# Two transformer blocks on one NeuronCore: attention steps regrouped among the products of the convolution units

## What is computed

```python
def hybrid_mixer(h, w_in, ...):
    proj = h @ w_in                      # 28 column groups of 128, and 8 gate columns
    aq, ak, av, dn_qkv, dn_z, dn_b, dn_a = jnp.split(proj, cuts, axis=-1)
    attn_out = dilated_attention(rope(aq), rope(ak), av)      # 8 heads of 64
    qkv = jax.nn.silu(causal_dwconv(dn_qkv, dn_conv_w))       # 12 of the 28 groups
    o = gated_delta_rule(dq, dk, dv, beta, g)
    return jnp.concatenate([attn_out, dn_out], axis=-1) @ w_out
```

## Time and profile before

| | |
|---|---|
| time, median of 3 runs | 2760.77 us (2760.47 to 2763.85) |
| the profiled execution's own time | 2765.85 us |
| its span | 2764.1 us (1.75 us lie around it) |
| TensorE busy | 97% of the span |
| ScalarE, VectorE, GpSimd busy | 40%, 40%, 44% |
| chain of work that ended last | 87% TensorE, 61% the unit's matmul line L1961 |
| conv units 13 to 23 in the trace | about 104 to 207 us (layer one), 742 us later again (layer two) |

### The profile page before, as it was taken

How to read it: one execution, slowest core, us unless ns; L and a number is a source line. 1 busy time by engine, 2 the same in 40 slices (tenths; PEclk the granted TensorE clock), 3 DMA queues, 4 the chain that set the end, 5 groups by cost and what they waited for, 6 DMA issues and landing times.

```text
span 2764.1 us, 42821 instructions
## 1 busy us (share of the span) xinstructions
PE 2685.1 (97%) x15208; PEld 2112.3 (76%) x15208; DVE 1098.6 (40%) x2260; ACT 1102.5 (40%) x1871; POOL 1211.5 (44%) x630
## 2 busy tenths in 40 slices
PE   9999999999999999999999999999999999999997
PEld 7767777888877677788887666788888666788886
DVE  4455454441154553644402586510113586510112
ACT  4454254443345533544434235532333235532331
POOL 3323235555433232355544452464653452364653
PEclk9999999999999999999999999999999999999998
DMA  3211023333322100233232221133332221133332
GB/s 136 77 54 40 9 77 91 99 93 105 106 71 69 54 25 24 78 97 96 94 106 92 71 69 47 62 99 99 92 98 84 71 69 47 61 97 94 99 93 97
DMA packets 62867, 217.16 MB, mean 79 GB/s; under 512 B 6576, under 2 KB 6704, under 8 KB 62480
## 3 DMA queue, kind: packets, MB, share of 16 engines
q1 hardware_dynamic: 62416, 214.28, 24.7%
q0 software_dynamic: 320, 1.12, 0.2%
HBM read 213.28 MB, written 2.10 MB: 78 GB/s over the span
## 4 chain that ended last, share of the span: by engine, by line
PE 87%; DVE 5%; ACT 2%; issue 2%; DVEq 2%; POOL 1%; DMA 0%; ACTq 0%; SPq 0%; POOLq 0%
PE bank L1961 61%; PE bank L2337 3%; PE bank L2011 3%; PE bank L2190 2%; PE bank L2191 2%; PE bank L2192 2%; PE bank L2023 1%; PE bank L2222 1%; PE bank L2234 1%; PE bank L2245 1%; PE bank L2127 1%; PE bank L1995 1%; PE bank L2356 1%; DVE mT L1786 1%; PE bank L1988 1%
## 5 line engine op out<-in xcount | busy, mean ns | idle before, releaser
L788 POOL TENSOR_TENSOR wL<-raw,wH 128x1024 fp32r<-128x1024 f32 x371 | 893.1, 2408 | 1085.5 <-ACT wH L977 1085.4
L1961 PE MATMUL bank<-hH,wH 128*128 128x512 f32 x1680 | 679.8, 405 | 7.0 <-DVE mT L1786 4.2
L1961 PE MATMUL bank<-hL,wH 128*128 128x512 f32 x1680 | 657.9, 392 | 0.0
L1961 PE MATMUL bank<-hH,wL 128*128 128x512 f32 x1680 | 657.5, 391 | 0.0
L977 ACT ACTIVATE wH<-raw 128x1024 fp32r<-128x1024 f32 x371 | 392.2, 1057 | 531.1 <-PE bank L1961 490.8
L1961 PEld LDWEIGHTS bank<-hH,wH 128*128 128x128 f32 x1680 | 317.1, 189 | 102.4 <-issue 28.8
L1961 PEld LDWEIGHTS bank<-hH,wL 128*128 128x128 f32 x1680 | 317.3, 189 | 67.5 <-issue 6.0
L1961 PEld LDWEIGHTS bank<-hL,wH 128*128 128x128 f32 x1680 | 316.9, 189 | 67.8
L1961 PE MATMUL bank<-hidH,wH 128*128 128x512 f32 x864 | 336.7, 390 | 0.0
L1961 PE MATMUL bank<-hidH,wL 128*128 128x512 f32 x864 | 336.2, 389 | 0.0
L1961 PE MATMUL bank<-hidL,wH 128*128 128x512 f32 x864 | 336.1, 389 | 0.0
(11 more groups left out here) (378 smaller groups left out, 3629.9 us busy)
## 6 DMA issues: line engine op xcount, KB each, us to landing
raw<-w_dram SPq DMA_DIRECT2D x398, 512.0 KB, 3.5
x<-x_dram SPq DMA_DIRECT2D x4, 512.0 KB, 9.6
out_dram<-x SPq DMA_DIRECT2D x1, 2048.0 KB, 6.3
const<-const_dram SPq DMA_DIRECT2D x1, 1229.0 KB, 13.2
par_next<-par_dram POOLq DMA_DIRECT2D x5, 168.0 KB, 3.5
qkT<-pos_dram POOLq DMA_DIRECT2D x1, 256.0 KB, 7.3
const<-const_dram SPq DMA_DIRECT2D x1, 131.0 KB, 2.2
```

The source lines that it names most:

```text
L788: pool.tensor_tensor(wL[:, s, :], raw[:, s, :], wH[:, s, :].bitcast(F32), ALU.subtract).then_inc(w_lo.sem, 1)
L1961: mm = pe.matmul((out or ACC[bk])[:, :], wt[:, c:c + P], rhs, start=first and k == 0 and j == 0, stop=last and k == tiles - 1 and j == 2)
```

## The change

TensorE's table of steps for a conv unit comes from a function instead of the fixed places 0, 3 and 6, and a place may hold more than one step. ScalarE's and VectorE's programs are not touched.

```diff
+def steps_in(v):
+
+    if v not in ATT_AT:
+        return {}
+    a, b, c = ATT_AT[v]
+    return {1: (a, b), 6: (c,)} if a % 2 else {0: (a,), 4: (b, c)}
...
-                    if k in after:
-                        attention(w, after[k])
+                    for n in after.get(k, ()):
+                        attention(w, n)
...
-                             after=dict(zip((0, 3, 6), ATT_AT.get(u, ()))))
+                             after=steps_in(u))
```

## The result

The changed kernel takes 2778.63 us (median of 5 runs, 2775.34 to 2778.71); the kernel before took 2762.91 us in the same session (5 runs, 2760.47 to 2767.95). The ratio is 1.0052 with a 95% interval of 1.0041 to 1.0063: by the ratio, slower by 14.4 us, 11.3 to 17.4 (the two medians are 15.7 us apart). The forecast was 14.0 us more, 2774.8 us, in a range of 2767 to 2783.

A forecast was written before the change was run, and what follows sets the result against it. TensorE, busy 104.1 of 105 us in each attention stage, was taken as the bound; even units 5.26 plus odd units 1.74 gave 7.00 us a layer, 14.0 in all, on 2760.8: 2774.8 us, range 2767 to 2783.

The forecast's parts named there:

- What bounds the stage: Attention stages: TensorE works 104.1 of 105 us in each, so whatever it waits in addition goes on the end.
- An even unit grows by its six products less the air: Units 14 to 22: six products of 0.23 us, 1.38 us, less each unit's air; 5.26 us a layer.
- The air method: Even units: second transposes' old start less copy's end plus 0.14 us; air of 0.01 to 0.40 us.
- Unit 22's old waits: Units 22 and 23: old waits of 0.46 and 0.18 us absorbed, so unit 22's 1.37 us becomes 0.73.
- Odd units: Pair behind k = 4: 0.57 us in unit 13, 0.92 in 23, 0.25 in the other four; 1.74 a layer.
- new neighbours: At each pair: coming to the scores from transposes instead of from a product costs about 0.03 us.
- Hidden: Even units: ScalarE's copy comes ahead of the pair, so the wait vanishes; 2760.2 us, no change; 5 in 100.
- Fewer breaks in the stream: One place less in each unit saves a toll, 22 x 0.22 = 4.8 us; 2754.7 us; 3 in 100.
- The clock falls: Behind the fourteen new waits the clock falls, 1.3 us each; all of them 18 us more, 2793; 8 in 100.
- The sum: Both layers' attention stages: 5.26 + 1.74 = 7.00 us a layer, 14.0 us in all, 2774.8 us, 0.5% slower.

The follow-up runs named there:

- odd-units kernel: Against the changed kernel, even units go back to steps behind k = 0, 3 and 6; only odd units keep the pair, behind k = 4: 2768.72 us, ratio 1.0019.
- two kernels with as many places as the change and few waits: Against the changed kernel: pairs behind k = 3 (even) and 6 (odd), 2766.61 us; ScalarE's weight high part moved behind its first attention step, 2768.81 us.
- the kernel with waits up to 0.82 us: Against the changed kernel, even pairs behind k = 0, odd units as before the change, ScalarE's weight high part behind its first attention step: 2771.77 us, ratio 1.0031.
- the kernel of before with ScalarE's edit: Against the kernel before, only ScalarE's high part of the weight moved behind the first attention step of its slots: 2762.23 us, ratio 1.0000.
- The kernel with the even units alone: Against the changed kernel, odd units go back to steps behind k = 0, 3 and 6; even units keep the pair behind k = 1: 2774.05 us, ratio 1.0037.

## Why the prediction was right, point by point

**What bounds the stage.** Right: TensorE, with no air. Every wait that the change made went on the end; nothing of it came back.

**An even unit grows by its six products less the air.** Right to 0.02 us in four units of five. The air method needs two rows of before for each unit, the end of the copy plus 0.14 us and the start of the transposes. It assumed that ScalarE's chain stays in place. The copy of unit 16 shows it, and the edit that moved the copy by 0.94 us took as much off the waits.

**Unit 22's old waits.** The largest error, 0.73 forecast and 0.54 measured, 0.4 us in two layers. I gave back what stood in the brackets, 0.46 + 0.18. Start to start the first was worth 0.66. The place with the four transposes of the earlier trace rows took from 193.70 to 195.25 us, 1.09 us more than two products; with the same transposes and no wait it took from 198.37 to 199.26 us in the changed trace, 0.43 us more.

**Odd units.** Units 13 and 23 right to 0.03 us. The odd-units kernel shows them alone. The 0.25 for the other four was 0.10: 0.09 in unit 19, where I had 0.13, and next to nothing in the three others, where I had 0.12 for new neighbours.

**The rivals.** *Hidden* is refuted: seven waits a layer. *Fewer breaks in the stream* is refuted by two kernels with as many places as the change and few waits (4.1 and 5.8 us slower, where the rows show 3.2 and 3.8 us of added waits and steps); a place less was worth 0.05 us a unit at most, not 0.22. The Trainium skill, "Perfetto Trace Analysis", section "Matmul Optimizations", asks for matmuls back to back in batches; longer batches are what these two kernels had, at no more than those 0.05 us. *The clock falls* did not happen in the change, with fourteen waits of 0.33 to 1.43 us and 1.00 behind each. But the forecast's reason, long streams of products between the waits, is not a sound one: three products earlier, with the same streams, it fell behind 13 of 20 waits of 1.3 to 1.75 us. The Trainium skill, "TensorE: Matmul & The Clock Gate", section "A second HAM failure mode: psum-queue depth-cycling", has the clock go up and down on short idle times between groups of matmuls; the rows of those kernels agree with it, those of the change and of the kernel with waits up to 0.82 us don't. The change's longest wait, 1.43 us, lies among the lengths behind which the clock fell elsewhere, so that none fell behind it was in part luck, and the chance of 8 in 100 was no overstatement. The price of a fall, 1.3 us, was too low. The stretch of the earlier trace rows begins 0.8 us ahead of the fall; laid on it, the trace of before shows the full depth:

```profile
425.00:428.40 3.40, 3.40 (x10) 2.65 (x9) 1.78 (x3) 1.04 (x2) 2.38 (x1) 0.50 0.00 0
```

A fall measured by itself took 1.6 us.

**The sum.** 14.0 us forecast, 13.2 in the two traces' stages, 14.4 timed. The forecast of 2774.8 stands 3.8 us below the measured median mostly because the runs of before in that session had a median 2.1 us above the one it was made on. Of the span's 12.8 us, the stages are +13.2, and the way to them is -1.7, nearly all of it a clock fall that only the trace of before has. Another fall, between the layers, only the trace of the changed kernel has. Its clock there, and the same sixteen small matmuls of both traces (one record of them is missing), first before, then changed:

```profile
385.50:388.90 3.40, 3.29 (x16) 3.21 (x17) 1.81 (x6) 1.38 (x3) 1.30 (x2) 0.51 0.66 205
```

```profile
380.95 2.05 PE L1995 MATMUL bank<-const,root 128*128 128x128 f32 x16
...
385.71 3.47 PE L2003 MATMUL bank<-const,root 128*128 128x128 f32 x15
```

The instructions of the changed kernel stand 4.8 us later than before ahead of this place and 6.0 us later behind it: +1.2. The rest, under 0.5 us net, is not placed; both traces have more falls behind it, at partly different places. The fall at 385.5 us is not shown to come from the change: the kernel of before with ScalarE's edit has one at its place too, at 379.2 us.

## What to carry to other kernels

Before two pieces of work on one buffer are put side by side, read how much air the second has: its start less the end of the copy that frees the buffer. What is taken from between them beyond that air comes back as a wait; here it did so within 0.02 us in four units of five. Where it must be done, first move what stands ahead of the copy on the copying engine; that was worth 8.6 us here, and nothing that the times could tell in the kernel where the air was there. And where such a wait comes to the 1.3 us and more behind which the clock fell here, price it with a possible fall on top, not by its length alone.

## What the runs showed of the hardware that was not expected

One and the same wait may or may not be followed by a fall of the clock. In the first layer, ahead of the attention stage, both kernels wait 1.97 us for GpSimd. First the kernel before, its timeline and then the stretch behind; then the changed one likewise:

```profile
52.46 0.50 PE L1961 MATMUL bank<-hH,wH 128*128 128x512 f32 x1 [1.97 <-POOL wL L788]
...
52.50:55.90 3.40, 3.40 (x9) 2.67 (x10) 1.14 (x2) 0.00 (x0) 2.68 (x1) 0.56 0.48 154
```

```profile
52.37 0.50 PE L1969 MATMUL bank<-hH,wH 128*128 128x512 f32 x1 [1.97 <-POOL wL L796]
...
52.40:55.80 3.40, 3.40 (x15) 2.81 (x16) 1.15 (x2) 0.00 (x0) 2.72 (x1) 1.00 0.52 154
```

Nine products in 3.4 us against fifteen, with the same instructions around. This also gives the price of one fall: the two traces are 0.09 us apart at this wait and 1.68 us apart at the start of the attention stage (103.95 and 102.27 us), so it took 1.6 us. The other eight kernels have the same wait of 1.96 or 1.97 us; the clock fell behind it in two of them (the odd units alone, and all pairs with the even ones behind `k` = 0) and not in six. Over the kernels with the pairs behind `k` = 0 the wait of 1.31 us was followed by a fall twice in four times, 1.53 twice, 1.40, 1.60 and 1.75 three times each; 1.43 and 1.20 in the change never, twice each. All twenty of the former had 0.2 to 0.3 us of idle time ahead of the scores as well, which those of the change had not. The kernel with the even units alone agrees with the change: ten waits of 0.91 to 1.40 us, without that idle time, and no fall. So a wait of 1.40 to 1.43 us was followed by a fall in none of four cases without the idle time, and in three of four with it. Whether that or chance makes the difference stays open. Nor is a long wait needed: in the 9 us ahead of the fall at 385.5 us TensorE's timeline shows no wait, and its last 2 us are sixteen matmuls with a single column (128x1). And single traces of this kernel differ by some 1.6 us for each fall without any cause in the code.
